# TensorE's loop over expert pairs written out, and the cross-attention's value products copied out in halves

## The chip, the cores and the metric

The kernel runs on one core of a Trainium2 chip. The metric is the device time of one execution in microseconds, as a median over runs. TensorE (PE in the rows; its weight loads are PEld) multiplies, VectorE (DVE) and ScalarE (ACT) move and transform what it leaves in PSUM, GpSimd (POOL) builds a few masks, and SyncE (SP) issues nearly all DMA transfers.

## What is computed

One decoder block over 256 tokens of width 1024, all in float32 at the interface:

```
x = x + parallel_mixer(rms_norm(x))                      # block-sparse attention and gated DeltaNet
x = x + memory_cross_attention(rms_norm(x), rms_norm(mem))
x = x + moe_ffn(rms_norm(x))                             # 32 experts, the best 4 for each token
return rms_norm(x)

# memory_cross_attention: 4 heads of 128, 256 memory tokens
p = softmax(q @ k.T * 128 ** -0.5);  o = p @ v;  return o @ w_o
# moe_ffn, for one expert and the tokens that chose it
gu = xb @ w_gate_up[e] + b_gate_up[e]                    # 1024 x 2048
act = (up + 1) * gate * sigmoid(1.702 * gate)            # gate, up clipped at 7
y = act @ w_down[e] + b_down[e]                          # 1024 x 1024
```

The experts' weights are 32 times 12 MB, and each of them is read once.

## The kernel before, in words

**Stages.** Each engine runs its own program and waits on semaphores. The first stage is the mixer, the second the cross-attention (names that begin with `x_`), then come the router and the experts. The experts are taken in 16 pairs, numbered 0 to 15 here. A pair has 12 chunks of weights of 2 MB: chunks 0 to 3 and 4 to 7 are `w_gate_up` of its two experts, 8 to 11 `w_down` of both. The chunks lie in ten places of SBUF, six of them the `ring` and four in `work`. SyncE waits until TensorE has given a place free (`slot_free`) and issues the next chunk's transfer. For pairs 0 to 4 and 15 each transfer is one chunk; for pairs 5 to 14 the chunks (1, 2), (5, 6), (8, 9) and (10, 11) come as 4 MB in one transfer (`load_twin`, L471). In the last pair, chunks 9 to 11 are cut into parts of 1 MB and 0.5 MB (L516 to L520).

**TensorE in a pair** (`pair_of_experts`, L2184). Gate and up products of both experts (L2119), the turning of their activations (L1588), the down products (L2166: one row of the timeline for two chunks, or for one where something is waited for), the sum into the tokens' rows (`combine`, L2181), and the gather of the next pair's tokens (L2097). `first_pass` (L2248) writes out pairs 0 to 4, runs pairs 5 to 13 as a hardware loop of 3 turns of 3 pairs each (`pe.Fori`, L2255), in which the values waited for are computed in registers (`pe.snap`), and writes out pairs 14 and 15. Ahead of the loop stand 36 waits on a semaphore that has long reached its value (L2253, L2254). VectorE, ScalarE and SyncE have loops of their own over the pairs, which the change does not touch.

**The cross-attention's end.** For each half of the tokens (t = 0, 1) TensorE turns the probabilities (`x_probs_turn`, L1588 in the rows), VectorE copies them out (L1252), TensorE multiplies them with the values, head after head (`x_pv`, L1931), ScalarE copies the result to `oT` (`x_pv_moved`, through `evacuate`, L588), and TensorE multiplies it with `w_o` (`x_out`, L1946: 8 products, n = 0 to 7, of which each takes two passes, so two rows' instructions). `x_out(0, ...)` has `x_probs_turn(1)` in it ahead of n = 4 and `x_pv(1)` ahead of n = 7; `x_out(1, ...)` has the first steps of the router in it. PSUM has 8 banks of 512 columns; a job owns a pair of neighbouring banks. `x_pv` writes the four heads side by side, 128 columns each, into the first bank of its pair. `take` waits until a pair is free, `drained` until it has been copied out.

**What starts the stream of expert weights.** Ten chunks are loaded as soon as the places of the mixer's and the cross-attention's weights come free. Every later chunk waits for TensorE to use up a chunk.

Of the kernel before, what the change touches and what calls it, by code (L numbers as in the profile page):

```python
# [24 lines left out]
P = 128  # L25
# [25 lines left out]
TURN_PAIRS = 3  # L51
TURN_USES = 4
BY_HALVES = 5
TURNS = 3
LOOP_FILLING = 36
BEHIND_TURNS = BY_HALVES + TURNS * TURN_PAIRS
FIRST_LOADS = [(0, 1), (0, 2), (0, 0), (0, 3), (0, 5), (0, 6), (0, 8), (0, 4), (0, 7), (0, 9)]
EPS = 1e-6
# [51 lines left out]
def bass_hybrid_block(nc, x, mem, norm_mix_g, w_in, gdn_conv_w, gdn_A_log, gdn_dt_bias, gdn_norm_g,  # L110
                      moba_norm_g, w_out, norm_xattn_g, norm_mem_g, xattn_w_q, xattn_w_kv, xattn_w_o,
                      norm_ffn_g, router_w, router_b, w_gate_up, b_gate_up, w_down, b_down, final_norm_g, out):
    with ExitStack() as ctx:
# [25 lines left out]
        oT = area(HT, KB, SEQ)  # L139
# [437 lines left out]
        def _(act):  # L577
# [161 lines left out]
                drain_done(last, f"x_score{t}")  # L739

            def x_pv_moved(t):
                evacuate(f"x_pv{t}", oT[:, 0:4, t * P:(t + 1) * P], blocks(f"x_pv{t}")[:, 0:4, :])

            x_query_moved(0)
            x_exp(0)
# [840 lines left out]
        def _(pe):  # L1586
# [338 lines left out]
            def x_pv(t):  # L1925
                name = f"x_pv{t}"
                drained(pe, f"x_probs_T{t}")
                take(pe, name)
                for h in range(GH):
                    for mt in range(TILES):  # L1930
                        last = nc.tensor.matmul(blocks(name)[:, h, :], vm_sb[:, mt, h * P:(h + 1) * P],  # L1931
                                                x_pT[:, 2 * h + mt, t * P:(t + 1) * P],
                                                start=(mt == 0), stop=(mt == TILES - 1))
                fill_done(last, name)

            def x_out(t, between):

                name = f"x_out{t}"
                wv = weights("x_o").rearrange("p (k n) -> p k n", n=D_MODEL)
                take(pe, name)  # L1940
                drained(pe, f"x_pv{t}")
                for n in range(2 * GH):
                    half, h = n // GH, n % GH
                    if n in between:
                        between[n](1)
                    last = nc.tensor.matmul(halves(name)[:, half, :], oT[:, h, t * P:(t + 1) * P],  # L1946
                                            wv[:, h, 512 * half:512 * half + 512],
                                            start=(h == 0), stop=(h == GH - 1))
                    if n == GH - 1:
                        last.then_inc(S("x_out_half"), 1)  # L1950
                fill_done(last, name)
# [44 lines left out]
            drained(pe, "mem_v")  # L1996
            x_pv(0)
            weights_landed(pe, "x_o")
            x_out(0, {4: x_probs_turn, 7: x_pv})
            def first_tile(_):  # L2000
                f_turn(0, 0, 4, 1)
                f_turn(0, 4, KB, 0)
# [245 lines left out]
            def first_pass():  # L2248
                gather_first()
                for i in range(BY_HALVES):  # L2250
                    pair_of_experts(0, i, i, 2 * i + 1, 2 * i + 2, lambda c: first_pass_chunk(i, c), (0, 0),
                                    opening=None if i else first_second_gather)
                for _ in range(LOOP_FILLING):  # L2253
                    pe.wait_ge(S("ident_ready"), 1)  # L2254
                with pe.Fori(0, TURNS) as rev:  # L2255
                    turned16 = pe.snap(rev * (16 * TURN_USES)), pe.snap(rev * (16 * TURN_PAIRS))
                    for q in range(BY_HALVES, BY_HALVES + TURN_PAIRS):
                        i = pe.snap(rev * TURN_PAIRS + q)
                        pair_of_experts(0, i, i, pe.snap(2 * i + 1), pe.snap(2 * i + 2),
                                        lambda c: first_pass_chunk(q, c), turned16)  # L2260
                for i in range(BEHIND_TURNS, PAIRS):
                    pair_of_experts(0, i, i, 2 * i + 1, 2 * i + 2, lambda c: first_pass_chunk(i, c), (0, 0),
                                    final=(i == PAIRS - 1), pieces=(i == PAIRS - 1))
# [45 lines left out]
```

## Time and profile before

| | |
|---|---|
| time, median of 3 runs | 1169.52 us (1169.34 to 1170.31) |
| the profiled execution's own time | 1169.5 us |
| its span | 1167.8 us |
| TensorE busy | 1096.4 us, 94% of the span |
| VectorE, ScalarE busy | 340.3 us (29%), 167.4 us (14%) |
| read from HBM | 433.95 MB, 373 GB/s over the span |
| transfers on SyncE's queue (q1) | 433.67 MB |
| queue q8, kind instruction | 36 transfers, 0.59 MB |

A busy engine isn't an engine at its peak, and a share over the span is an average over stages. The strips of the page cut the span into 40 slices of 29.2 us. The kind "instruction" is code that an engine fetches while it runs; it goes through the same 16 DMA engines as the weights.

### The profile page before, as it was taken

The page shows a single profiled execution, that of the slowest core. Times are in us where ns is not written, and L with a number is a line of the kernel's source. Part 1 is how long each engine was busy: PE and PEld are TensorE (multiplying, and loading weights), DVE is VectorE, ACT ScalarE, POOL GpSimd, SP SyncE. Part 2 cuts the span into 40 slices and gives each one's busy share as a digit, 9 for nine tenths or more (in the row PEclk, how much of TensorE's full clock was granted, in tenths as well). Part 3 has the DMA queues.
Part 4 walks back from the last instruction along what each step waited for, and adds up shares of the span by engine and source line. Part 5 has one row for each costly group of instructions (what it writes and reads, how often), then busy time and mean ns, then how long its engine had stood idle before and what let it go on. Part 6 is the DMA issues. An engine that isn't in the chain of part 4 may idle for free.

```text
span 1167.8 us, 14131 instructions
## 1 busy us (share of the span) xinstructions
PE 1096.4 (94%) x5917; PEld 527.8 (45%) x5917; DVE 340.3 (29%) x740; ACT 167.4 (14%) x275; POOL 3.8 (0%) x22
## 2 busy tenths in 40 slices
PE   8999999999999999999898989898989898989897
PEld 8988884863434333333333332333333333333332
DVE  5792334362122222131313131313121212121213
ACT  3521235340000001010101010101010101010002
POOL 1000000000000000000000000000000000000000
PEclk9999999999999999999998999999989899999999
DMA  9842314869999999999999999999999999999995
GB/s 339 312 144 78 141 72 117 360 240 430 426 429 429 427 426 428 429 429 433 425 433 425 436 424 436 426 436 425 436 426 435 427 434 427 435 427 434 423 426 236
DMA packets 40198, 435.67 MB, mean 373 GB/s; under 512 B 5957, under 2 KB 6042, under 8 KB 20474
## 3 DMA queue, kind: packets, MB, share of 16 engines
q1 hardware_dynamic: 38234, 433.67, 88.5%
q10 hardware_dynamic: 1920, 1.34, 0.6%
q8 instruction: 36, 0.59, 0.2%
q14 instruction: 8, 0.07, 0.0%
HBM read 433.95 MB, written 1.05 MB: 373 GB/s over the span
## 4 chain that ended last, share of the span: by engine, by line
PE 65%; DMA 32%; ACT 1%; DVE 1%; SPq 1%; issue 1%; DVEq 0%; PEldq 0%
DMA ring<-in_w_down 31%; PE ps L2119 19%; PE ps L2166 17%; PE ps L2181 4%; PE ps L1750 4%; PE ps L1606 4%; PE ps L1696 3%; PE ps L2097 3%; PE ps L1588 2%; PE ps L1746 2%; PE ps L1799 2%; PE ps L1902 1%; PE ps L1946 1%; PE ps L2054 1%; ACT work L812 1%
## 5 line engine op out<-in xcount | busy, mean ns | idle before, releaser
L2166 PE MATMUL ps<-ring,work 128*64 128x512 f32 x1024 | 241.9, 621 | 38.6 <-DMA ring<-in_w_down 35.5
L2119 PE MATMUL ps<-ring,work 128*64 128x512 f32 x1024 | 229.1, 600 | 9.5 <-DMA ring<-in_w_gate_up 9.5
L2119 PE MATMUL ps<-work 128*64 128x512 f32 x1024 | 230.5, 592 | 0.0
L2166 PEld LDWEIGHTS ps<-ring,work 128*64 128x64 f32 x1024 | 79.3, 142 | 176.3 <-issue 156.9
L2119 PEld LDWEIGHTS ps<-ring,work 128*64 128x64 f32 x1024 | 72.4, 138 | 161.2 <-issue 143.7
L2119 PEld LDWEIGHTS ps<-work 128*64 128x64 f32 x1024 | 71.8, 137 | 135.7 <-issue 129.3
L1459 DVE TENSOR_SCALAR work<-ps 128x512 f32<-128x512 f32 x32 | 22.0, 686 | 201.0 <-PE ps L1588 201.0
L1482 DVE COPY work<-ps 128x512 f32<-128x512 f32 x16 | 11.1, 691 | 221.2 <-PE ps L1588 221.2
L1494 DVE COPY work<-ps 128x512 f32<-128x512 f32 (+1 forms) x16 | 11.1, 691 | 216.8 <-PE ps L2166 216.8
L2181 PE MATMUL ps<-work 128*128 128x512 f32 (+1 forms) x132 | 59.7, 607 | 10.4 <-ACT work L812 10.2
L805 ACT ACTIVATE ps<-work 128x512 f32<-128x512 f32 x32 | 19.2, 601 | 340.1 <-DVE work L1459 340.1
L807 ACT COPY work<-ps 128x512 f32<-128x512 f32 x32 | 18.7, 585 | 317.1 <-PE ps L1588 317.1
L1588 PEld LDWEIGHTS ps<-small,work 128*128 128x128 f32 (+1 forms) x338 | 41.6, 167 | 44.5 <-issue 41.7
L1588 PE MATMUL ps<-small,work 128*128 128x128 f32 (+1 forms) x338 | 54.0, 289 | 1.0 <-DVE work L875 1.0
L1475 DVE TENSOR_TENSOR work<-work,ps 128x1024 f32<-128x1024 f32 x30 | 36.6, 1221 | 38.0 <-PE ps L2181 38.0
L2097 PEld LDWEIGHTS ps<-work 128*128 128x128 bf16 x720 | 41.5, 106 | 8.6 <-issue 8.6
L2181 PEld LDWEIGHTS ps<-work 128*128 128x128 f32 (+1 forms) x132 | 22.9, 189 | 48.0 <-issue 23.8
L1750 PE MATMUL ps<-ring,work 128*128 128x256 f32 x192 | 43.9, 382 | 0.0
L1606 PE MATMUL ps<-work,ring 128*128 128x256 f32 x192 | 42.9, 380 | 0.0
L2097 PE MATMUL ps<-work 128*128 128x128 bf16 x720 | 42.6, 219 | 0.0
L1606 PEld LDWEIGHTS ps<-work,ring 128*128 128x128 f32 x192 | 35.9, 190 | 5.4 <-issue 0.8
L1750 PEld LDWEIGHTS ps<-ring,work 128*128 128x128 f32 x192 | 35.5, 190 | 5.3 <-issue 0.7
(253 smaller groups left out, 744.3 us busy)
## 6 DMA issues: line engine op xcount, KB each, us to landing
work<-in_w_gate_up SPq DMA_DIRECT2D x64, 2048.0 KB, 36.3
ring<-in_w_gate_up SPq DMA_DIRECT2D x20, 4096.0 KB, 32.7
ring<-in_w_down SPq DMA_DIRECT2D x20, 4096.0 KB, 37.2
ring<-in_w_gate_up SPq DMA_DIRECT2D x24, 2048.0 KB, 23.7
ring<-in_w_down SPq DMA_DIRECT2D x21, 2048.0 KB, 23.5
ring<-in_w_in SPq DMA_DIRECT2D x6, 2048.0 KB, 18.5
ring<-in_xattn_w_kv SPq DMA_DIRECT2D x2, 2048.0 KB, 14.4
ring<-in_w_out SPq DMA_DIRECT2D x2, 2048.0 KB, 8.0
```

Source lines behind the costliest of these rows:

```text
L1459: nc.vector.tensor_scalar(gate_sb, bank(GATE_BANK[k]), LIMIT, None, ALU.min) \
L1475: nc.vector.tensor_tensor(x_sb[:, t, :], x_sb[:, t, :], ps[:, 512 * b:512 * b + 1024], ALU.add).then_inc(S("combined"), 1)
L1588: return nc.tensor.transpose(dst, src, ident[0:n_in, 0:n_in])
L1606: last = nc.tensor.matmul(pair(name)[:, SEQ * b:SEQ * b + SEQ], w[:, k, b * P:(b + 1) * P], moving[:, k, :], start=(k == 0), stop=(k == KB ...
L1696: return nc.tensor.matmul(dst, still, moving, start=True, stop=True)
L1746: last = nc.tensor.matmul(pair(name)[:, SEQ * q:SEQ * q + SEQ], w[:, k, q * P:(q + 1) * P], hT[:, k, :], start=(k == 0), stop=(k == KB - 1))
L1750: last = nc.tensor.matmul(halves(name)[:, t, c:c + 256], tokens[:, k, t * P:(t + 1) * P], w[:, k, c:c + 256], start=(k == 0), stop=(k == K ...
L1799: last = nc.tensor.matmul(halves(f"mix_out{t}")[:, half, :], oT[:, k, t * P:(t + 1) * P], wv[:, k, :], start=(k == 4), stop=(k == 3))
L2097: last = nc.tensor.matmul(dst, split[s][:, t, columns], picks[:, t, :], start=(s == 0 and t == 0), stop=(s == 2 and t == TILES - 1))
L2119: last = nc.tensor.matmul(bank(b)[p], xg_T[k][:, kb, :], quad_columns(w[:, kk, D_MODEL * (q // 2):D_MODEL * (q // 2 + 1)], q % 2), start=F ...
L2166: last = nc.tensor.matmul(bank(Y_BANK + y)[p], act_T[k][:, b, HALF * c:HALF * c + HALF], w[:, b, 512 * q:512 * q + 512], start=False, stop ...
L2181: return nc.tensor.matmul(bank(COMBINE_BANK[t] + q), g_T[rows, q, P * t:P * t + P], y_sb[rows, q, :], start=start, stop=stop)
```

## The change

It has two parts. The first pass's loop over pairs 5 to 13 on TensorE is written out with constants in place of registers, and the 36 waits ahead of it are gone. In the cross-attention, `x_pv` puts heads 0 and 1 into the first bank of its pair and heads 2 and 3 into the second; ScalarE copies the two halves with two instructions, the first as soon as head 1 is done (`x_pv_half`); `x_out` begins when the first half has been copied (`x_pv_half_moved`) and waits for the second ahead of n = 2; and `x_probs_turn(1)` stands ahead of n = 5 rather than n = 4.

```diff
--- before.py
+++ after.py
@@ -52,7 +52,6 @@
 TURN_USES = 4
 BY_HALVES = 5
 TURNS = 3
-LOOP_FILLING = 36
 BEHIND_TURNS = BY_HALVES + TURNS * TURN_PAIRS
 FIRST_LOADS = [(0, 1), (0, 2), (0, 0), (0, 3), (0, 5), (0, 6), (0, 8), (0, 4), (0, 7), (0, 9)]
 EPS = 1e-6
@@ -739,7 +738,10 @@
                 drain_done(last, f"x_score{t}")
 
             def x_pv_moved(t):
-                evacuate(f"x_pv{t}", oT[:, 0:4, t * P:(t + 1) * P], blocks(f"x_pv{t}")[:, 0:4, :])
+                name, mine = f"x_pv{t}", slice(t * P, (t + 1) * P)
+                act.wait_ge(S("x_pv_half"), t + 1)
+                nc.scalar.copy(oT[:, 0:2, mine], blocks(name)[:, 0:2, :]).then_inc(S("x_pv_half_moved"), 1)
+                evacuate(name, oT[:, 2:4, mine], blocks(name)[:, 4:6, :])
 
             x_query_moved(0)
             x_exp(0)
@@ -1928,9 +1930,12 @@
                 take(pe, name)
                 for h in range(GH):
                     for mt in range(TILES):
-                        last = nc.tensor.matmul(blocks(name)[:, h, :], vm_sb[:, mt, h * P:(h + 1) * P],
+                        last = nc.tensor.matmul(blocks(name)[:, 4 * (h // 2) + h % 2, :],
+                                                vm_sb[:, mt, h * P:(h + 1) * P],
                                                 x_pT[:, 2 * h + mt, t * P:(t + 1) * P],
                                                 start=(mt == 0), stop=(mt == TILES - 1))
+                    if h == 1:
+                        last.then_inc(S("x_pv_half"), 1)
                 fill_done(last, name)
 
             def x_out(t, between):
@@ -1938,9 +1943,11 @@
                 name = f"x_out{t}"
                 wv = weights("x_o").rearrange("p (k n) -> p k n", n=D_MODEL)
                 take(pe, name)
-                drained(pe, f"x_pv{t}")
+                pe.wait_ge(S("x_pv_half_moved"), t + 1)
                 for n in range(2 * GH):
                     half, h = n // GH, n % GH
+                    if n == 2:
+                        drained(pe, f"x_pv{t}")
                     if n in between:
                         between[n](1)
                     last = nc.tensor.matmul(halves(name)[:, half, :], oT[:, h, t * P:(t + 1) * P],
@@ -1996,7 +2003,7 @@
             drained(pe, "mem_v")
             x_pv(0)
             weights_landed(pe, "x_o")
-            x_out(0, {4: x_probs_turn, 7: x_pv})
+            x_out(0, {5: x_probs_turn, 7: x_pv})
             def first_tile(_):
                 f_turn(0, 0, 4, 1)
                 f_turn(0, 4, KB, 0)
@@ -2250,14 +2257,11 @@
                 for i in range(BY_HALVES):
                     pair_of_experts(0, i, i, 2 * i + 1, 2 * i + 2, lambda c: first_pass_chunk(i, c), (0, 0),
                                     opening=None if i else first_second_gather)
-                for _ in range(LOOP_FILLING):
-                    pe.wait_ge(S("ident_ready"), 1)
-                with pe.Fori(0, TURNS) as rev:
-                    turned16 = pe.snap(rev * (16 * TURN_USES)), pe.snap(rev * (16 * TURN_PAIRS))
+                for rev in range(TURNS):
                     for q in range(BY_HALVES, BY_HALVES + TURN_PAIRS):
-                        i = pe.snap(rev * TURN_PAIRS + q)
-                        pair_of_experts(0, i, i, pe.snap(2 * i + 1), pe.snap(2 * i + 2),
-                                        lambda c: first_pass_chunk(q, c), turned16)
+                        i = rev * TURN_PAIRS + q
+                        pair_of_experts(0, i, i, 2 * i + 1, 2 * i + 2, lambda c: first_pass_chunk(q, c),
+                                        (16 * TURN_USES * rev, 16 * TURN_PAIRS * rev))
                 for i in range(BEHIND_TURNS, PAIRS):
                     pair_of_experts(0, i, i, 2 * i + 1, 2 * i + 2, lambda c: first_pass_chunk(i, c), (0, 0),
                                     final=(i == PAIRS - 1), pieces=(i == PAIRS - 1))
```

TensorE's instructions at the cross-attention's end, from the products with the values of the first tokens to the first product of `x_out(1, ...)`. The names in square brackets are semaphores; `pair_drained3` says that the pair of banks of `x_pv0` (and before it of others) is copied out. Before:

```order
L1931 MATMUL ps<-work 128x128 x7
L1946 MATMUL ps<-ring,work 128x512 [waits pair_drained3,pair_drained0,slot_loaded0]
L1946 MATMUL ps<-ring,work 128x512 x3
L1588 MATMUL ps<-small,work 128x128 [waits x_probs_ready,pair_drained1]
L1588 MATMUL ps<-small,work 128x128 x7
L1946 MATMUL ps<-ring,work 128x512 x3
L1931 MATMUL ps<-work 128x128 [waits pair_drained2,pair_drained1]
L1931 MATMUL ps<-work 128x128 x7
L1946 MATMUL ps<-ring,work 128x512
L1946 MATMUL ps<-ring,work 128x512 [waits pair_drained2,pair_drained3]
```

and with the change (its lines are numbered 2 to 7 higher):

```order
L1933 MATMUL ps<-work 128x128 x7
L1953 MATMUL ps<-ring,work 128x512 [waits x_pv_half_moved,pair_drained0,slot_loaded0]
L1953 MATMUL ps<-ring,work 128x512
L1953 MATMUL ps<-ring,work 128x512 [waits pair_drained3]
L1953 MATMUL ps<-ring,work 128x512 x2
L1590 MATMUL ps<-small,work 128x128 [waits x_probs_ready,pair_drained1]
L1590 MATMUL ps<-small,work 128x128 x7
L1953 MATMUL ps<-ring,work 128x512 x2
L1933 MATMUL ps<-work 128x128 [waits pair_drained2,pair_drained1]
L1933 MATMUL ps<-work 128x128 x7
L1953 MATMUL ps<-ring,work 128x512
L1953 MATMUL ps<-ring,work 128x512 [waits x_pv_half_moved,pair_drained3]
```

The wait for the whole copy has become a wait for its half, the other one stands a product pair later, and the turning of the second probabilities has moved behind one more product (which is two instructions at run time).

ScalarE's instructions at the same place, before:

```order
L736 ACTIVATE work,small<-ps,small 128x256 [waits pair_filled0,x_bias_ready]
L736 ACTIVATE work,small<-ps,small 128x256 x3
L588 COPY work<-ps 128x4x128 [waits pair_filled3] x2
L736 ACTIVATE work,small<-ps,small 128x256 [waits pair_filled1,x_bias_ready]
L736 ACTIVATE work,small<-ps,small 128x256 x3
L594 ACT_TABLE_LOAD
L594 ACTIVATE small<-small 128x1
L588 COPY work<-ps 128x4x128 [waits pair_filled2,table_loaded]
```

and with the change:

```order
L735 ACTIVATE work,small<-ps,small 128x256 [waits pair_filled0,x_bias_ready]
L735 ACTIVATE work,small<-ps,small 128x256 x3
L587 COPY work<-ps 128x4x128 [waits pair_filled3]
L743 COPY work<-ps 128x2x128 [waits x_pv_half]
L587 COPY work<-ps 128x2x128 [waits pair_filled3]
L735 ACTIVATE work,small<-ps,small 128x256 [waits pair_filled1,x_bias_ready]
L735 ACTIVATE work,small<-ps,small 128x256 x3
L593 ACT_TABLE_LOAD
L593 ACTIVATE small<-small 128x1
L743 COPY work<-ps 128x2x128 [waits x_pv_half,table_loaded]
L587 COPY work<-ps 128x2x128 [waits pair_filled2]
```

Each copy of 4 times 128 columns has become two of 2 times 128 columns; nothing has changed its place in the order.

TensorE's instructions where pair 4 ends and pair 5 begins, before:

```order
L2097 MATMUL ps<-work 128x128 [waits picked]
L2097 MATMUL ps<-work 128x128 x47
L2255 UNCONDITIONAL_BRANCH [waits ident_ready]
L2255 ISA
L2188 REGISTER_ALU [waits expert_chosen]
L2054 MATMUL ps<-work,small 64x512 [waits combined]
L2054 MATMUL ps<-work,small 64x512 x3
L2104 ISA [waits gathered]
L2119 MATMUL ps<-work 64x512 [waits slot_loaded6]
L2119 MATMUL ps<-work 64x512 x7
```

and with the change:

```order
L2104 MATMUL ps<-work 128x128 [waits picked]
L2104 MATMUL ps<-work 128x128 x47
L2061 MATMUL ps<-work,small 64x512 [waits combined,expert_chosen]
L2061 MATMUL ps<-work,small 64x512 x3
L2126 MATMUL ps<-work 64x512 [waits slot_loaded6,gathered]
L2126 MATMUL ps<-work 64x512 x7
L2126 MATMUL ps<-ring,work 64x512 [waits slot_loaded5]
L2126 MATMUL ps<-ring,work 64x512 x7
```

The branch, the register instructions and the filling waits are gone, and the products are the same. Further on, the 172 products of a pair stand nine times in the program where they stood three times.

## Rows read from the trace of the kernel before

**Rows 1.** The page, parts 1 and 2; slices of 29.2 us.

```profile
PE 1096.4 (94%) x5917; PEld 527.8 (45%) x5917; DVE 340.3 (29%) x740; ACT 167.4 (14%) x275; POOL 3.8 (0%) x22
...
DMA  9842314869999999999999999999999999999995
GB/s 339 312 144 78 141 72 117 360 240 430 426 429 429 427 426 428 429 429 433 425 433 425 436 424 436 426 436 425 436 426 435 427 434 427 435 427 434 423 426 236
```

**Rows 2.** Waits of TensorE: us in total, times, longest us.

```profile
PE ps L2166 <- DMA ring<-in_w_down: 35.5, 15, 3.2
...
PE ps L2119 <- DMA ring<-in_w_gate_up: 9.5, 7, 2.5
```

**Rows 3.** The chain of waits, ends of pairs 1 and 2: start, us.

```profile
356.65 3.70 PE ps L2181 x8
...
409.59 3.70 PE ps L2181 x8
```

**Rows 4.** Timeline of TensorE, down products: start, us, what, [idle before, releaser].

```profile
617.10 6.45 PE L2166 MATMUL ps<-ring,work 128*64 128x512 f32 x16 [3.16 <-DMA ring<-in_w_down]
...
675.43 3.65 PE L2166 MATMUL ps<-ring,work 128*64 128x512 f32 x16 [2.94 <-DMA ring<-in_w_down]
...
735.51 3.65 PE L2166 MATMUL ps<-ring,work 128*64 128x512 f32 x16 [1.47 <-DMA ring<-in_w_down]
...
1086.09 5.35 PE L2166 MATMUL ps<-ring,work 128*64 128x512 f32 x16 [3.17 <-DMA ring<-in_w_down]
```

**Rows 5.** Timeline of the weight loads (PEld) at the last chunk's last part.

```profile
1154.69 0.14 PEld L2166 LDWEIGHTS ps<-ring,work 128*64 128x64 f32 x2 [0.38 <-DMA ring<-in_w_down]
```

**Rows 6.** Stretch: busy us by engine, granted clock, DMA share, GB/s.

```profile
256.00:258.00 2.00, 2.00 (x12) 0.62 (x10) 1.74 (x5) 1.97 (x6) 0.00 (x0) 1.00 0.00 0
```

**Rows 7.** Timeline of SyncE's issues, the next chunk after that stretch.

```profile
259.45 0.33 SPq L469 DMA_DIRECT2D work<-in_w_gate_up  x1
```

**Rows 8.** The chain of waits, cross-attention's end: start, us, what.

```profile
225.20 1.80 PE ps L1931 x16
...
227.02 0.59 ACT work L588
...
227.75 3.67 PE ps L1946 x8
...
238.57 0.87 PE ps L1588 x8
...
245.96 1.72 PE ps L1946 x4
```

**Rows 9.** Timeline of all engines there.

```profile
229.68 1.23 DVE L1246 TENSOR_TENSOR work<-work,small 128x1024 f32<-128x1024 f32 x1
...
232.33 1.23 DVE L1252 COPY work<-ps 128x1024 f32<-128x1024 f32 x1 [1.42 <-PE ps L1588]
...
236.75 0.58 ACT L588 COPY work<-ps 128x512 f32<-128x512 f32 x1 [5.80 <-PE ps L1931]
```

**Rows 10.** A copy of 256 columns by ScalarE: ns min/median/max, first and last start.

```profile
L617 ACT COPY work<-ps x1: 372/372/372, 25.8 to 25.8; 128x256 f32<-128x256 f32 x1
```

**Rows 11.** DMA queue q8, 476 to 692 us: transfers, MB, share.

```profile
q8 instruction: 8, 0.13, 0.2%
```

**Rows 12.** The same, 700 to 1040 us; there is no other queue.

```profile
q1 hardware_dynamic: 6723, 146.57, 100.5%
```

**Rows 13.** The same in the 4 us from 688 us on.

```profile
q8 instruction: 1, 0.02, 1.7%
```

**Rows 14.** SyncE's issues of two transfers: start, us, what.

```profile
438.36 0.33 SPq L469 DMA_DIRECT2D ring<-in_w_gate_up  x1
...
441.80 0.33 SPq L469 DMA_DIRECT2D ring<-in_w_gate_up  x1
```

**Rows 15.** The same two transfers: size, us from issue to landing.

```profile
ring<-in_w_gate_up SPq DMA_DIRECT2D x1, 2048.0 KB, 30.8
...
ring<-in_w_gate_up SPq DMA_DIRECT2D x1, 2048.0 KB, 33.8
```

## The prediction

> **What bounds the kernel now.** I read the page's strips first. TensorE is busy for 94% of the span, which suggests that it is the bound; but from slice 11 on the DMA share stands at 9 tenths or more and the rate at 423 to 436 GB/s up to the slice before last [rows 1]. The reader is to see two numbers that both look full. The waits decide between them: TensorE waits 35.5 us for `w_down` and 9.5 us for `w_gate_up` [rows 2]. The chain tells why not from the start: pair 2 ended 52.94 us after pair 1 (409.59 - 356.65) [rows 3], without a wait for a transfer. A pair's weights take longer: the wait for chunk 8 ended at 735.51 and, six pairs on, at 1086.09, so 58.43 us for each [rows 4]. TensorE is 5.5 us a pair faster than the transfers, has eaten up the stock of ten chunks within the first pairs, and from pair 5 on it waits in every pair. To the very end: its last weight load before the combine still waits for the last part of chunk 11 [rows 5]. So the end is the landing of the last weights and a fixed tail of some 13 us. That landing is where the full stream begins plus the time that it takes. It begins where TensorE gives its first chunk free: between 256 and 258 us the DMA engines are idle [rows 6], and the next chunk is issued at 259.45 [rows 7]. Two questions decide the change: does TensorE reach that point earlier, and does the stream take longer or shorter.
>
> **Part 1, the copy in halves.** In the chain, the products with the values (start 225.20, 1.80 us) end at 227.00, ScalarE's copy of 0.59 us follows, and the next products begin at 227.75: 0.75 us in which TensorE stands [rows 8]. The eight instructions after it take 3.67 us. Four later ones, at 245.96 and without a stop ahead of them, took 1.72 us, or 0.43 each, so eight would be 3.44 [rows 8]: the other 0.23 I take as the pipeline filling up again, an estimate from these two rows. With the change the first half (heads 0 and 1) is ready some 0.9 us earlier, at about 226.1. ScalarE copied 256 columns in 0.37 us elsewhere [rows 10], so the first half is out at about 226.5, before TensorE is through with heads 2 and 3, and it goes on at 227.0. The second half begins at 227.0, is out at 227.4, and is wanted at n = 2, 1.7 us after 227.0. So 0.75 and 0.23 go.
>
> What is late next? The second tokens' probabilities were ready at 229.68 + 1.23 = 230.91 [rows 9]. TensorE would now reach the old place of their turning, n = 4, at 227.0 + 3.44 = 230.4 and wait 0.5 us; at n = 5 it comes at 231.3 and doesn't. ScalarE's exponentials stand behind the copies; two copies of 0.37, of which the first lies under TensorE's products, end 0.2 us earlier than one of 0.59, so they are no later. VectorE's copy of the turned probabilities (start 232.33, 1.23 us [rows 9]) starts 0.1 us earlier and ends near 233.5; the second `x_pv` wants it at 231.3 + 0.87 + 1.72 = 233.9. It fits by 0.4 us. At the second copy (start 236.75, 0.58 us [rows 9]) TensorE lost another 0.2 us; that goes too. By this sum the first product of `x_out(1, ...)` ends at 237.4, where it was 238.57 [rows 8]: 1.2 us. Behind it VectorE and ScalarE work in a chain on what TensorE ended, and both start as much earlier. I take 1.1 us as what reaches the issue at 259.45; the bounds are 0 (VectorE or ScalarE sets the pace on the way) and 1.2. The two more copies and waits lie beside TensorE's products.
>
> **Part 2, the waits and the loop's own instructions.** The 36 waits, the branches and the registers take TensorE's time at pair 5's beginning and at each turn. All of it lies ahead of a wait for a transfer, which gets longer by as much (pair 6 waits 3.16 us at chunk 8 [rows 4]). Worth 0, and no more than 0, since the ending wait is a landing.
>
> **Part 3, the code.** What the page shows beside the weights is q8: TensorE's code, which the same 16 DMA engines carry. Between 476 and 692 us there were 8 transfers [rows 11]. Between 700 and 1040, the second and third turn, there was none: q1 is the only queue [rows 12]. The loop's body is fetched once and then kept. Written out, six pairs more are fetched: two turns at about 6.5 transfers each (8 in 216 us is one in 27 us, three pairs are 175.3 us), so 13 more.
>
> What does one cost? As bytes, 13 times 16 KB are 0.2 MB, 0.5 us at 430 GB/s. But one transfer of code lies on one DMA engine: in the 4 us from 688 it took 1.7% of 16 engines, 1.1 us of a single one [rows 13]. All 16 engines are full, a chunk has landed when the last of them is through, and an engine that lost 1 us never gets it back. So what counts is the engine that is most behind. The rows fit this. Pair 6's chunk 8 to pair 7's is 58.33 us, although code was fetched in between; pair 7's to pair 8's is 60.08 [rows 4], 1.65 more, around the transfer at 688, after which the pace is 58.43 again and nothing is caught up. The same step stands once more: the transfer issued at 438.36 landed 30.8 us later at 469.2, the next one, issued at 441.80, landed 33.8 us later at 475.6 [rows 14, 15]. That is 6.4 us for 2 MB, where 58.43 / 12 = 4.87 is the pace: 1.5 more. Between these two steps lie just the 8 transfers of [rows 11]. I read it so: code goes round eight DMA engines, the same one is always most behind, and each eighth transfer makes the whole stream 1.6 us longer, while the seven between are free.
>
> With 13 more transfers, one each 27 us after 688, the next such steps come at about 905 and 1120. The last weights land at about 1155, so both count, the second for the last seven chunks only, and there TensorE has no slack left [rows 5]. Cost: 2 times 1.57 (the mean of 1.65 and 1.5) = 3.15 us. The bounds are 0 (if the steps have another cause) and 4.7 (a third step, if the count is shifted).
>
> Here the Trainium skill speaks for the change. Its page Runtime: NRT & Kernel Launch, section Instruction fetch mechanics, says that code comes in blocks of 16 KiB, that fetching them is mostly hidden, that nothing is kept but what was fetched ahead in order, and that full unrolling is preferred. The size agrees with the trace. That nothing is kept doesn't: a loop of three pairs ran two turns without a fetch. That it is hidden holds for TensorE, which never waited for code; by that rule the sum would be that of the first rival.
>
> **The sum.** The profiled execution took 1169.5 us (span 1167.8 and 1.7 around it), as good as the median of 1169.52. 1169.5 - 1.1 - 0 + 3.15 = 1171.55; I say 1171.5, or 0.17% slower.
>
> **Rivals.** About 0.2% (2.3 us) is what a measurement of this kernel can tell from no change.
> First, code is free: the steps at 475 and 690 came from something else (a chance of the memory). For it: two events are few, and in seven of eight transfers nothing is seen. Then only the copy counts: 1169.5 - 1.1 = 1168.4.
> Second, slower beyond doubt: the gain of the copy is lost between 238 and 255 us. VectorE is the place: in a fixed order it sums, turns and splits what TensorE leaves for the router, and if one of these instructions waits for something that didn't move, TensorE's 1.1 us are waited away ahead of the first expert; it decides from 0.3 us of lost gain on. With the code's 3.15: 1169.5 + 3.15 = 1172.65. Against it: the chain of waits runs on TensorE nearly all the way there.
> Third, only one step counts, because the second comes after the last weights' issue or hits an engine with room: 1169.5 - 1.1 + 1.57 = 1170.0.
> Fourth, all code rides on one engine, each transfer costs 1.57: 13 times 1.57 less 1.1, 1188.8. Against it: 58.33 us with code in between.
> A remainder is that neither part counts, 1169.5.
>
> **How the numbers follow.** Forecast 0.50, first rival 0.14, second 0.13, third 0.15, fourth 0.02, the remainder 0.06. Within the forecast the two sizes are known to some 0.7 us together, and 1171.9 is the bound of slower, so three in ten of it lie beyond: 0.15, with the second and fourth rival 0.29. Faster is below 1167.2, which only the first rival's low end reaches: 0.05. The rest, 0.66, is within 0.2%. The range is 1168.2 to 1172.7; it takes in the first and the second rival.
>
> **What would show it.** Right, if the issue at 259.45 comes near 258.3 and TensorE shows no stop between `x_pv` and `x_out`; if q8 has about 49 transfers in place of 36, spread through 700 to 1040 us; and if the waits for chunk 8 stand 58.4 us apart except for two distances of 60, at pair 8 and near pair 11, with a third step in the last pair. Wrong in part 1, if the first step of the router ends earlier but the issue doesn't; wrong in part 3, if 13 more transfers of code come and all distances stay 58.4. TensorE waiting for code would be wrong altogether.

## The result, and the profile after

| | median us | lowest to highest | runs |
|---|---|---|---|
| before | 1170.63 | 1169.24 to 1173.04 | 16 |
| with the change | 1172.26 | 1171.26 to 1173.94 | 16 |

The ratio is 1.0017, with an interval of 1.001 to 1.0023: slower by 0.17%, which is 2.0 us, where 0.17% was forecast (the two medians lie 1.63 us apart, inside the interval). The profiled execution took 1171.51 us (span 1169.7), 2.0 us more than the 1169.5 of before; single executions of one kernel differ by as much, so that agreement is partly luck.

From the page with the change: busy time by engine, the strips of the DMA engines (40 slices), and the DMA queues (packets, MB, share of 16 engines).

```profile
PE 1098.6 (94%) x5917; PEld 530.5 (45%) x5917; DVE 340.4 (29%) x740; ACT 168.0 (14%) x277; POOL 3.9 (0%) x22
...
DMA  9842314869999999999999999999999999999995
GB/s 339 311 144 77 140 72 118 359 259 429 429 426 428 425 427 429 429 428 433 425 434 426 434 427 435 425 433 426 431 428 433 429 432 428 433 426 431 427 426 215
...
q8 instruction: 49, 0.80, 0.3%
```

The reader sees the picture of [rows 1] again: nothing there gives away two microseconds. What changed is q8, the code: 49 transfers. (In the forecast that was 36 and 13 more.)

The chain of waits at the changed place, to be held against [rows 8]: start, length, engine, line, instructions.

```profile
225.36 1.78 PE ps L1933 x16
227.15 4.29 PE ps L1953 x10
231.44 0.87 PE ps L1590 x8
232.31 1.72 PE ps L1953 x4
234.03 1.78 PE ps L1933 x16
235.82 1.72 PE ps L1953 x4
237.54 1.01 PE ps L1590 x8
238.55 2.58 PE ps L1953 x6
```

And the instruction with which SP starts the stream of weights, for [rows 7].

```profile
258.55 0.33 SPq L468 DMA_DIRECT2D work<-in_w_gate_up  x1
```

The products with the values (L1933) are followed by `x_out`'s (L1953) at once: ScalarE's copy is out of the chain at both places, and ten instructions take 4.29 us, 0.43 each. From the start of the first product with the values to SP's issue it was 34.25 us before (259.45 - 225.20) and is 33.19 now (258.55 - 225.36), so 1.06 us are gained. One small thing was not forecast: the eight turnings at 237.54 take 1.01 us instead of 0.87. They come earlier and wait for VectorE (L1283), 0.14 us of the gain.

The first down products of chunk 8 in five of the ten pairs that were read, to be held against [rows 4]: start, length, then in brackets the idle time ahead and who ended it.

```profile
674.79 5.35 PE L2173 MATMUL ps<-ring,work 128*64 128x512 f32 x16 [3.01 <-DMA ring<-in_w_down]
734.60 3.65 PE L2173 MATMUL ps<-ring,work 128*64 128x512 f32 x16 [1.46 <-DMA ring<-in_w_down]
...
851.47 3.65 PE L2173 MATMUL ps<-ring,work 128*64 128x512 f32 x16 [3.02 <-DMA ring<-in_w_down]
...
911.42 5.30 PE L2173 MATMUL ps<-ring,work 128*64 128x512 f32 x16 [4.52 <-DMA ring<-in_w_down]
...
1086.74 6.38 PE L2173 MATMUL ps<-ring,work 128*64 128x512 f32 x16 [2.90 <-DMA ring<-in_w_down]
```

And TensorE's last wait for a weight, to be held against [rows 5].

```profile
1156.88 0.20 PEld L2173 LDWEIGHTS ps<-ring,work 128*64 128x64 f32 x4 [0.89 <-DMA ring<-in_w_down]
```

734.60 - 674.79 is 59.81 us and 911.42 - 851.47 is 59.95; the other seven distances between pairs 5 and 14 lie between 58.40 and 58.62. The last stretch, 1086.74 to 1156.88, is 70.14 us, where it was 1154.69 - 1086.09 = 68.60 before. So with the change there are two steps more than before. The first is 1.56 us: from 734.60 to 1086.74 it is 352.14 us, and from 735.51 to 1086.09 it was 350.58. The second is 1.54 us, in the last stretch. The sum for the stream: the stream begins 0.90 us earlier (258.55 for 259.45) and ends 2.19 us later (1156.88 for 1154.69); -0.90 + 1.56 + 1.54 = 2.20.

The kernel's end does not follow the stream alone. Here are TensorE's last 32 down products and the first combine products behind them, before and then with the change.

```profile
1148.96 7.09 PE L2166 MATMUL ps<-ring,work 128*64 128x512 f32 x32
1156.20 1.14 PE ps L2181 x4
...
1150.64 7.32 PE L2173 MATMUL ps<-ring,work 128*64 128x512 f32 x32
1158.12 1.14 PE ps L2188 x4
```

Before, TensorE waited for no transfer after chunk 8 of pair 14. The wait of [rows 5] is 0.38 us of the weight loads where 0.26 is their usual gap, and it held up no product. With the change the last four products came with the weights at 1156.88, 0.24 us late. The end moved by 1158.12 - 1156.20 = 1.92 us. Of these, 0.65 us were there at chunk 8 of pair 14 (1086.74 for 1086.09) and 0.24 came from the last landing. The other 1.03 us are a lower clock: the 16 products behind that wait took 6.38 us and before 5.35, where 3.65 is their time at full clock. The granted clock from 1085 to 1092 us was 0.53 and 0.76. By the records of the packets the last weights' packet ended 0.46 us ahead of the last combine with the change (1157.66), and 0.72 us ahead of it before (1155.48). So in both kernels the landing and TensorE's own work end within 0.3 us of each other, an estimate from these two distances.

### The profile page after: what moved, and what is told of

It reads as the page before. It is cut to its first block, busy times and chain, and to the rows that moved or that the text cites. A ratio compares the mean times of both kernels' runs of the same rounds, so it can differ in the third digit from the quotient of the medians.

```text
span 1169.7 us, 14069 instructions
## 1 busy us (share of the span) xinstructions
PE 1098.6 (94%) x5917; PEld 530.5 (45%) x5917; DVE 340.4 (29%) x740; ACT 168.0 (14%) x277; POOL 3.9 (0%) x22
## 4 chain that ended last, share of the span: by engine, by line
PE 64%; DMA 32%; ACT 1%; DVE 1%; SPq 1%; issue 1%; DVEq 0%; PEldq 0%; ACTq 0%
DMA ring<-in_w_down 32%; PE ps L2126 19%; PE ps L2173 18%; PE ps L1752 4%; PE ps L1608 4%; PE ps L2188 4%; PE ps L1698 3%; PE ps L1590 3%; PE ps L1748 2%; PE ps L1801 2%; PE ps L2104 2%; PE ps L1904 1%; PE ps L1953 1%; PE ps L2061 1%; DMA work<-in_mem 1%
## 5 line engine op out<-in xcount | busy, mean ns | idle before, releaser
L1752 PEld LDWEIGHTS ps<-ring,work 128*128 128x128 f32 x192 | 35.5, 190 | 5.3 <-issue 0.7
```

What stands on the lines that cost most here:

```text
L1752: last = nc.tensor.matmul(halves(name)[:, t, c:c + 256], tokens[:, k, t * P:(t + 1) * P], w[:, k, c:c + 256], start=(k == 0), stop=(k == K ...
```

## The experiments

All are compared with the kernel before, run beside them. The **theory** is the prediction's: the copy in halves gains about 1.1 us, the code that is fetched costs by steps of about 1.6 us, one for eight transfers, and the 36 waits cost nothing as time. The **rivals**: code costs by the byte or not at all; the waits or the loop do something else than take time.

### e1_copy_alone: only the copy in halves

```diff
+LOOP_FILLING = 36
...
-                for rev in range(TURNS):
+                with pe.Fori(0, TURNS) as rev:
```

(The kernel with the change, with the loop and its waits put back.)

> The copy in halves alone; the loop and its 36 waits as before. My theory (one transfer of code in eight lengthens the stream by 1.57 us): code transfers as before, 36, so the same steps as before, near 475 and 690 us and none behind; the stream's first issue near 258.5 instead of 259.45; the end 0.9 us earlier, ratio 0.9992 against the kernel before. Rival (the copy's gain is lost on the way): ratio 1.0000, the issue at 259.4.

Measured: 1168.99 us (1168.2 to 1170.42, 11 runs), beside 1169.98 of before; ratio 0.9989 [0.998, 0.9998]. The issue, two of the distances and the end of the stretch in its trace:

```profile
258.44 0.33 SPq L469 DMA_DIRECT2D work<-in_w_gate_up  x1
```

```profile
674.88 5.17 PE L2174 MATMUL ps<-ring,work 128*64 128x512 f32 x16 [3.27 <-DMA ring<-in_w_down]
734.75 5.35 PE L2174 MATMUL ps<-ring,work 128*64 128x512 f32 x16 [3.16 <-DMA ring<-in_w_down]
...
910.11 5.32 PE L2174 MATMUL ps<-ring,work 128*64 128x512 f32 x16 [3.17 <-DMA ring<-in_w_down]
...
1085.47 6.38 PE L2174 MATMUL ps<-ring,work 128*64 128x512 f32 x16 [2.96 <-DMA ring<-in_w_down]
```

One step (59.87 us at 734.75), no other; six pairs from 734.75 to 1085.47 are 350.72 us, 58.45 each. By the ratio the copy in halves alone brings 0.11%, some 1.3 us, with an interval from 0.2 to 2.3. The profiled execution (1169.9 us) doesn't show that gain at its end. The issue is 1.01 us earlier and chunk 8 of pair 14 is 0.62 us earlier, but then the clock is lower than before (6.38 us for the 16 products in place of 5.35), and the last combine begins 0.4 us later than before:

```profile
1156.60 1.14 PE ps L2189 x4
```

### e2_loop_out_alone: only the loop written out

```diff
-LOOP_FILLING = 36
...
-                with pe.Fori(0, TURNS) as rev:
+                for rev in range(TURNS):
```

> The loop written out and its waits gone, the copy as before. My theory: 49 transfers of code, steps of 1.5 to 1.6 us near 475, 695, 905 and 1122 us, two more than before, and a ratio of 1.0027 (3.15 us). Rival (the steps are a chance of the memory): steps elsewhere or in another number than with the changed kernel, and a ratio anywhere from 1.000 to 1.003.

Measured: 1173.95 us (1172.26 to 1174.49, 7 runs); ratio 1.0031 [1.002, 1.0043], some 3.6 us. q8 between 700 and 1040 us:

```profile
q8 instruction: 12, 0.20, 0.2%
```

```profile
676.30 5.35 PE L2165 MATMUL ps<-ring,work 128*64 128x512 f32 x16 [3.02 <-DMA ring<-in_w_down]
735.40 5.04 PE L2165 MATMUL ps<-ring,work 128*64 128x512 f32 x16 [3.15 <-DMA ring<-in_w_down]
...
852.48 3.65 PE L2165 MATMUL ps<-ring,work 128*64 128x512 f32 x16 [3.06 <-DMA ring<-in_w_down]
912.30 5.34 PE L2165 MATMUL ps<-ring,work 128*64 128x512 f32 x16 [3.92 <-DMA ring<-in_w_down]
```

```profile
1157.72 0.20 PEld L2165 LDWEIGHTS ps<-ring,work 128*64 128x64 f32 x4 [1.05 <-DMA ring<-in_w_down]
```

The step at 912 is there again, 59.82 us, and so is the one at the end (69.96 from chunk 8 of pair 14, 1087.76, to 1157.72). The step near 690 came in two parts: 59.04 up to 676.30 and 59.10 up to 735.40, each about 0.65 over the pace, 1.3 together. Here the 16 products behind 1087.76 ran at full clock (3.65 us), and TensorE did wait for the last landing, so that the second step reached the end. The two parts of the change, -1.3 and +3.6, give +2.3 together; 2.0 were measured for both.

### e3_no_waits: the loop kept, its 36 waits taken away

```diff
-LOOP_FILLING = 36
+LOOP_FILLING = 0
```

> Only the 36 waits ahead of the loop are taken out of the kernel before. My theory: all they took lies ahead of a wait for a transfer, so the time stays (ratio 1.0000, within 0.0005), with 36 transfers of code and three steps. Rival (the waits put the loop's body where it is kept between turns): without them code is fetched in the second and third turn as well, 8 or more transfers more, and the ratio is 1.0013 or 1.0027.

Measured: 1172.99 us (1172.38 to 1173.88, 8 runs); ratio 1.0026 [1.0015, 1.0037]. My expectation of no difference fell and the rival stood: with nothing ahead of it, the body of the loop is no longer kept from turn to turn. From q8 between 700 and 1040 us, from the waits between 300 and 1160 us (total, times, longest), and from the timeline behind the first turn:

```profile
q8 instruction: 17, 0.28, 0.3%
```

```profile
PE ps L2166 <- DMA ring<-in_w_down: 20.7, 10, 3.2
PE ps L2054 <- issue: 10.6, 2, 5.4
PE ps L2119 <- issue: 6.1, 2, 3.2
```

```profile
706.57 1.07 PE L2054 MATMUL ps<-work,small 96*64 96x512 bf16 x4 [5.43 <-issue]
```

TensorE now stands for 5.4 us at a turn and 3.2 us soon after it, waiting for nothing but its own instructions. Yet these 16.7 us are not what costs: its waits for `w_down` shrink beside them (20.7 us, where the kernel before had 35.5 [rows 2]). The loss is where the theory has it, in the stream: from the first issue to the last weights it takes 1158.00 - 259.62 = 898.38 us where it took 895.24 before (1154.69 - 259.45), two steps' worth. The rows for chunk 8 show them: 677.18, 854.00 and 1030.86 are three pairs apart each, 176.8 us, where three pairs at the pace are 175.3. There were five transfers more than with the change, at other times, and still only two more steps than before.

### e4_one_turn_out: two turns in the loop, the third written out

```diff
-                for rev in range(TURNS):
+                with pe.Fori(0, TURNS - 1) as rev:
...
+                for rev in (TURNS - 1,):
```

(With the copy in halves and the 36 waits.)

> The changed kernel, but two turns stay in the loop (with its 36 waits) and only the third, pairs 11 to 13, is written out. My theory (the engine that the first transfer of code behind the stream's start went to gets each eighth one): 42 or 43 transfers of code, none between 700 and 870 us; steps near 475 and 690 as before, none near 905, one more near 1075; the time is 1.57 - 0.9 = 0.7 us over the kernel before, ratio 1.0006. Rival (every transfer costs the same, 0.2 us): about the same time, but no step anywhere. Rival (steps come at fixed times): a step near 905.

Measured: 1170.98 us (1169.78 to 1173.17, 10 runs); ratio 1.0008 [0.9999, 1.0018]. q8 between 870 and 1130 us (from 700 to 870 it has no transfer), and the waits for chunk 8:

```profile
q8 instruction: 10, 0.16, 0.3%
```

```profile
909.20 5.35 PE L2174 MATMUL ps<-ring,work 128*64 128x512 f32 x16 [3.19 <-DMA ring<-in_w_down]
968.21 5.19 PE L2174 MATMUL ps<-ring,work 128*64 128x512 f32 x16 [3.16 <-DMA ring<-in_w_down]
1026.64 4.99 PE L2174 MATMUL ps<-ring,work 128*64 128x512 f32 x16 [3.18 <-DMA ring<-in_w_down]
1086.05 6.00 PE L2174 MATMUL ps<-ring,work 128*64 128x512 f32 x16 [3.96 <-DMA ring<-in_w_down]
```

This is the test in which the steps were moved. Without code in the second turn, the step by 911 is gone: 850.63 to 909.20 is 58.57 us. The next one comes where the count of transfers puts it: 59.41 us up to 1086.05, with 0.6 of it already at 968.21 (59.01). The two together are 1.56, split as in e2. One thing was expected otherwise: the step near 690 was to be as before, and is 0.6 us smaller (from 616.05 to 733.82 it is 117.77 us, where before had 118.41). So the 0.6 at 968.21 may be what was left over from it.

### e7_150_waits: before, with 150 waits in place of 36

```diff
-LOOP_FILLING = 36
+LOOP_FILLING = 150
```

> The kernel before with 150 waits ahead of the loop in place of 36 (75 instructions in place of 18). Rival (any shift away from the chosen number breaks it): code fetched in every turn, over 50 transfers, a stop of about 5 us at each turn's end, 1172.5 us or more.

A single run: 1169.8 us, span 1168.1. From the waits between 300 and 1160 us, and from the queues between 700 and 1040:

```profile
PE ps L2054 <- issue: 7.5, 1, 7.5
```

```profile
q1 hardware_dynamic: 6720, 146.54, 100.5%
```

7.5 us of waiting instructions on TensorE cost nothing to be seen, and the body is kept: q1 is the only queue in the later turns, as in [rows 12]. So the number of waits is free as time. Whether there are any decides if the body is kept. That this is a matter of where the body begins is my reading of 0, 36 and 150; the place itself isn't in the profile.

### e6_loop_from_2: copy in halves, four turns from pair 2 on

```diff
-BY_HALVES = 5
-TURNS = 3
+BY_HALVES = 2
+TURNS = 4
```

> The copy in halves, the loop kept with its 36 waits, and pairs 2 to 4 taken into it as well (4 turns of 3 pairs; their weights then come as 4 MB transfers too). My theory: 29 or 30 transfers of code, of which the 30th comes after the last weights, so the step near 690 is gone and only that near 475 stays: 1.57 us less than with the copy alone, ratio to before 0.9979. Rival (the larger transfers of pairs 2 to 4 leave the queue dry, since each waits for two places): idle DMA engines between 300 and 450 us, and no gain or a loss of up to 5 us.

Measured: 1176.56 us (1175.48 to 1179.5, 5 runs); ratio 1.0062 [1.0048, 1.0076]. This expectation fell altogether: I wanted less code, and got more. Waits between 300 and 1160 us, and a stretch of 2 us (busy time by engine, clock, DMA share, GB/s):

```profile
PE ps L2062 <- issue: 19.9, 4, 6.6
```

```profile
336.00:338.00 2.00, 2.00 (x12) 0.69 (x10) 0.00 (x0) 0.00 (x0) 0.00 (x0) 1.00 0.57 172
```

The body is fetched again in each turn (56 transfers in all), and TensorE stands four times, 5 us on average. Besides, I take the larger transfers from pair 2 on to wait for places that come free too late while TensorE is still the slower side: the DMA share falls to 0.57 (1.00 before, in the same 2 us). From 300 to 450 us the rate is 423 GB/s where it was 427, an estimate of 1.4 us; the rest of the loss isn't divided.

### e5_fill and e9_fill_less: with the change, TensorE made slower on purpose

```diff
+            if isinstance(i, int) and BY_HALVES <= i < BEHIND_TURNS:
+                for _ in range(142):
+                    pe.wait_ge(S("ident_ready"), 1)
```

(60 in place of 142 in e9_fill_less.)

> The changed kernel with 142 waits on a semaphore long reached ahead of each of pairs 5 to 13 (71 instructions a pair, 639 in all, 2.5 transfers of code, 4.3 us of TensorE's time a pair by the 1.1 us that 36 waits took). My theory: 51 or 52 transfers, the number of steps unchanged since the next eighth one would be the 54th, waits for weights shorter by 4.3 us a pair, and the end where it was, 1171.5 (or 1173, where the changed kernel's slower runs lie). Rival (TensorE's own instructions count): 9 times 4.3, 38 us more.

> The changed kernel with 60 waits ahead of each of pairs 5 to 13. By the 142 waits that took 6.7 us a pair these take 2.8 us, under the 5.5 us that TensorE has over in a pair, and add one transfer of code. My theory: 50 transfers, the 46th a little earlier than 1120 us, five steps as in the changed kernel, the last weights at 1156.5 to 1157.5 and the time as the changed kernel's, ratio to before 1.0015 to 1.003. Rival (a stop of 2.8 us lets the clock fall, and the two together are over the 5.5 us): 2 us or more on top.

Measured: e5_fill 1188.5 us (a single run); e9_fill_less 1171.64 us (1171.07 to 1173.87, 10 runs), ratio 1.0017 [1.0008, 1.0027]. The waits between 300 and 1160 us, first of 142, then of 60:

```profile
PE ps L2061 <- issue: 60.2, 9, 6.8
```

```profile
PE ps L2061 <- issue: 20.1, 9, 2.3
PE ps L2173 <- DMA ring<-in_w_down: 23.5, 13, 3.2
```

60 waits are 2.2 us a pair and vanish in the waits for `w_down`: the ratio is that of the change alone. 142 waits are 6.7 us a pair. I had sized them at 4.3; TensorE has 5.5 to spare, so they make it the bound, and it waits for no weights at all in these 860 us. From the combine of pair 6 (639.09) to that of pair 13 (1069.78) a pair takes 61.53 us. Its own work and the waits are 52.94 + 6.7 = 59.6. Beside the other 1.9 stands a lower clock (busy time by engine, the granted clock, DMA share, GB/s): 0.93 in this stretch, where the kernel with the change had 0.95, with TensorE idle for 15 of the 100 us.

```profile
700.00:800.00 100.00, 84.94 (x442) 34.00 (x442) 20.98 (x40) 6.71 (x9) 0.00 (x0) 0.93 1.00 424
```

At the combine of pair 13 e5_fill is 22.5 us behind the kernel with the change (1069.78 for 1047.24). Pair 14 has no filling, takes 52.92 us and gives 5.3 back, which leaves the 17 us. The two kernels enclose the 5.5 us that the prediction read from [rows 3, 4].

### e8_turn_at_4: copy in halves, turning at n = 4 as before

```diff
-            x_out(0, {5: x_probs_turn, 7: x_pv})
+            x_out(0, {4: x_probs_turn, 7: x_pv})
```

(On top of e1_copy_alone.)

> The copy in halves with the loop kept, but the second probabilities' turning at its old place, ahead of n = 4. My theory: TensorE comes there at 230.6 and waits 0.3 to 0.5 us for VectorE's product that is ready near 230.9; nothing else moves, so the stream's first issue comes 0.3 to 0.5 us later than with the copy alone (258.44), at 258.7 to 258.9. Rival (the step to n = 5 is worth nothing, since VectorE or ScalarE set the pace behind it): 258.4 again.

A single run: 1171.04 us, issue at 260.86. This chain, with the one of e1_copy_alone behind it:

```profile
225.78 1.80 PE ps L1934 x16
...
231.44 1.07 PE ps L1591 x8
...
238.58 1.01 PE ps L1591 x8
```

```profile
225.25 1.78 PE ps L1934 x16
...
237.42 1.02 PE ps L1591 x8
```

From the first product with the values to the third turning it is 12.80 us, where e1_copy_alone has 12.17. So 0.63 us are lost at the place where the prediction had a wait of 0.5. It explains a part only: this execution was 0.5 us later before it came there, and lost another 1.3 us behind it. That is the clock: in this execution TensorE's was lower around 252 us, in e1_copy_alone it was full (this one first, then e1_copy_alone):

```profile
252.00:256.00 4.00, 4.00 (x24) 3.36 (x20) 1.76 (x8) 0.62 (x1) 0.00 (x0) 0.68 0.64 266
...
252.00:256.00 4.00, 4.00 (x22) 3.16 (x23) 2.99 (x7) 2.03 (x3) 0.00 (x0) 1.00 0.38 156
```

## Why the prediction was right, point by point

**What bounds.** The landing of the weights, up to chunk 8 of pair 14: what began the stream earlier or made it longer moved that point in every run but e5, and what TensorE lost ahead of a wait did not (e7: 7.5 us once; e3: 16.7 us in all; e9: 2.2 us a pair). Behind that point the prediction was too simple. It read [rows 5] as TensorE without slack and put a fixed tail of 13 us behind the landing. In fact TensorE's own work is as late as the landing there, and from the combine of pair 14 to that of pair 15 it takes 52.4 us without a wait for a transfer in before, e1, e3, e4, e7, e8 and e9. Only with the change and in e2 does the last landing hold it up, by 0.24 and 1.3 us.

**Part 1.** 1.1 us forecast at the issue; 1.06 from the first product with the values on, 0.90 by absolute time, 1.01 in e1. At the last weights 0.64 us of e1's were left, by the records of the packets. The small loss to VectorE at the third turning (0.14 us) is the second rival's mechanism, on an eighth of its size. n = 5 for the turning was needed, by the single run of e8: with n = 4, 0.63 us are lost at that place.

**Part 2.** Nothing forecast, and right for this change, in which loop and waits go together. The reason was too narrow: I judged the waits as time only. They also decide whether the loop's body is kept, and by that they are worth 0.26% (e3), more than the copy in halves. Had the change taken away the waits and kept the loop, the same words would have forecast 0 where 3 us were lost.

**Part 3.** 13 more transfers forecast, 13 came; steps at about 905 and 1120, of 1.57 us each, forecast; the trace has them by 911 and behind 1087, of 1.56 and 1.54. Three runs speak for steps and against a price of each byte or transfer. The table has the stream from the first issue to the last wait for a weight.

| kernel | transfers of code | stream, us |
|---|---|---|
| before | 36 | 1154.69 - 259.45 = 895.24 |
| e4_one_turn_out | 43 | 1155.19 - 258.26 = 896.93 |
| with the change | 49 | 1156.88 - 258.55 = 898.33 |
| e2_loop_out_alone | 49 | 1157.72 - 259.56 = 898.16 |
| e9_fill_less | 50 | 1156.73 - 258.52 = 898.21 |
| e3_no_waits | 54 | 1158.00 - 259.62 = 898.38 |

The records of the weights' packets say the same, from the first behind the issue to the last: 895.06 us before, 895.43, 895.37 and 895.46 in e1, e7 and e8, which have 36 transfers too, and then 896.75, 898.13, 897.99, 898.00 and 898.21 in e4, with the change, e2, e9 and e3.

From 36 to 49 transfers the stream is 3.09 us longer, from 49 to 54 it is 0.05. At an even price of 3.09 / 13 = 0.24 us, the five last would have cost 1.2. "The seven between are free" was nearly right: where a step falls in two (e2, e4), I take two DMA engines to be about equally far behind, so that two transfers bring half of it each. Which engine carries which transfer isn't in the profile, but something in it repeats every eight. The single transfers of code, in order from 308 us on, lasted 1.10, 1.09, 1.02, 1.02, 1.07, 1.07, 1.06 and 1.10 us before, and then the same eight again. In every run whose stream stayed full, each lasted as long as the eighth before it, within 0.01 us almost everywhere. The row begins at another of the eight with the change than before, while the steps keep their count. So it isn't always the same engine that is behind. The count fits, within one transfer, the first one behind the stream's start and each eighth after it. That the eight are DMA engines remains a reading.

The Trainium skill says, on the page Runtime: NRT & Kernel Launch, section Instruction fetch mechanics, that a branch to a place outside what was fetched makes the engine wait for a fetch. With the stops of 5.2 and 5.4 us at the two turns of e3 this trace agrees. The same section prefers full unrolling; here the unrolled loop costs 0.31% (e2) against a loop whose body is kept, and the measurement decides. Against the loop without its waits it would cost next to nothing (1.0031 and 1.0026, intervals that overlap).

**The sum.** -1.1 + 3.15 = +2.05 us forecast, +2.0 by the ratio. For the stream it is right term by term. At the end of the profiled executions it is right in part by luck: there the second step is worth 0.24 us and a lower clock 1.03. The clock doesn't make the kernel slower by itself, since the landing alone would have ended it as late: in e2, at full clock, TensorE waits for the last weights and the step is there in full. The rivals are out: free code and a single step by the distances, the lost copy by the issue and the ratio of e1, code all on one engine by the seven distances of 58.4 us.

**Open.** The single executions of one kernel are spread over 2 to 4 us (before: 1169.24 to 1173.04), as much as the whole effect; no trace of a slow and a fast one of the same kernel says why. The clock behind chunk 8 of pair 14 is a candidate: the 16 products took 3.65 us in e2 and e7 and 5.1 to 6.5 in the others, and the combine of pair 14 came 17.48 us (e2) to 18.87 us (e9) after chunk 8, which nothing behind takes back. That is 1.4 us at most, so not all of the spread. The share of the two causes in e6 is open, and why a loop's body is kept or not.

**The better kernel** is e1_copy_alone: the copy in halves with the loop and its 36 waits kept, 0.9989 of before [0.998, 0.9998], and 3.3 us under the change as made (1168.99 for 1172.26, from different sets of runs).

## What to carry to other kernels

Where the DMA engines are full to the end, look at everything they carry beside the data: instructions too are a load, and a small transfer can be free seven times and cost 1.5 us the eighth. Look at the very last stage by itself: a wait that comes back in every pair says nothing of the last one, where a lower clock of TensorE can cost as much as a late landing. Before a loop is written out or a filler ahead of it is removed, see whether the code's queue is silent during the later turns; if it is, the loop's body is being kept, and that can be worth more than its instructions. And when a copy stands between two matmul groups, releasing its first half early takes it out of the chain, provided that whatever is interleaved behind it is moved back by as much.

## What the runs showed of the hardware

- A transfer of code (16 KB) takes 1.1 us of a single DMA engine [rows 13]; a stream at 430 GB/s gets 1.3 to 1.6 us longer about once in eight transfers, and nothing is caught up afterwards. In the totals of the page it is 0.3% of the queues' share. The transfers' durations repeat with a period of eight.
- A loop of three pairs of experts on TensorE is kept between its turns with 36 or 150 waits ahead of it (no transfer in 340 us), and is fetched again with none (17 transfers in 340 us), and in e6 with 36 and another start. A turn to code that isn't there cost 5.2 to 5.4 us at once and about 3 us more soon after (e3).
- Waits that are already fulfilled cost TensorE time, though not in proportion: 36 took 1.1 us, 60 took 2.2, 142 took 6.7, 150 took 7.5.
- Behind a wait of 2.9 to 4.0 us for weights, the same 16 products took 3.65 us at full clock (e2, e7) and up to 6.5 us in executions whose granted clock fell there (0.53 from 1085 to 1092 us with the change).
